# A three-part reordering of a two-block kernel: first norm with tokens on partitions, head products by rows, layer norm beside the gate tiles

## What is computed

```python
n = _rms(h, norm_mix_w[l])              # h: 528 x 1024
z = n @ w_in[l]                         # q, k, v, glu, g_att, g_conv
o = _diff_attention(q, k, v, lam, cid)  # 8 heads, two maps each, block-causal
y_att = _rms(o, subln_w[l]) * (1.0 - lambda_init)
u = glu[..., :CONV_CH] * jax.nn.sigmoid(glu[..., CONV_CH:])
u = _causal_dwconv(u, conv_dw_w[l], conv_dw_b[l])          # 31 taps
u = jax.nn.silu(_layernorm(u, conv_ln_w[l], conv_ln_b[l]))
y_conv = u @ w_conv_out[l]
m = jax.nn.sigmoid(g_att) * y_att + jax.nn.sigmoid(g_conv) * y_conv
h = h + m @ w_out[l]
h = h + conv_ffn(_rms(h, norm_ffn_w[l]))                   # then the second block
```

## Time and profile before

| | |
|---|---|
| median of 3 runs | 1731.55 us (1729.71 to 1734.51) |
| profiled execution | 1731.61 us, of it the span 1729.8 |
| TensorE busy | 1600.2 us, 93% |
| VectorE busy | 1166.5 us, 67% |
| ScalarE busy | 682.9 us, 39% |
| start, to the third chunk of products | 62.5 us |
| one turn of the heads | 36.8 us |
| turns 8 and 9, to the first chunk of w_conv_out | 426.3 to 520.2 us |

### The profile page before, as it was taken

One profiled execution on the slowest core, in us unless ns is written; L12 is line 12 of the kernel. 1 busy time (PEld: TensorE's weight loads), 2 busy tenths in 40 slices (PEclk: granted clock), 3 DMA queues, 4 the chain that ended last, 5 costly groups with the idle time before them and its releaser, 6 DMA issues.

```text
span 1729.8 us, 25539 instructions
## 1 busy us (share of the span) xinstructions
PE 1600.2 (93%) x9943; PEld 1408.4 (81%) x9943; DVE 1166.5 (67%) x1603; ACT 682.9 (39%) x1013; POOL 11.4 (1%) x26
## 2 busy tenths in 40 slices
PE   5997999999879999999999977979986899999996
PEld 4997889898779999999988866757865688888885
DVE  5889877876435578777764479855537887777334
ACT  3221455545453344433433344533633433343232
POOL 0000000000000000000000020000000000000000
PEclk8999999999999999999999998889998999999997
DMA  4232221121112323333223431312111333332331
GB/s 135 74 97 59 67 71 50 50 72 51 49 49 74 98 75 96 97 97 88 66 84 100 108 86 30 71 49 61 50 49 51 95 97 97 94 86 65 95 96 49
DMA packets 261145, 131.02 MB, mean 76 GB/s; under 512 B 21056, under 2 KB 259524, under 8 KB 261076
## 3 DMA queue, kind: packets, MB, share of 16 engines
q1 hardware_dynamic: 260692, 129.87, 27.2%
q0 software_dynamic: 384, 0.20, 0.0%
HBM read 127.95 MB, written 2.10 MB: 75 GB/s over the span
## 4 chain that ended last, share of the span: by engine, by line
PE 79%; DVE 14%; ACT 5%; issue 1%; DMA 0%; SPq 0%; DVEq 0%; ACTq 0%
PE psP L609 31%; PE psS L609 19%; PE psP L672 14%; PE psP L629 4%; DVE conv L1745 2%; DVE wl L1665 2%; PE psP L783 1%; DVE sc L2012 1%; DVE m L2011 1%; PE psS L745 1%; ACT wh L1175 1%; PE psP L1040 1%; PE psP L887 1%; PE psP L781 1%; DVE mT L2254 1%
## 5 line engine op out<-in xcount | busy, mean ns | idle before, releaser
L1665 DVE TENSOR_TENSOR wl<-raw,wh 128x2048 fp32r<-128x2048 f32 x130 | 297.9, 2291 | 151.8 <-ACT wh L1175 149.8
L609 PE MATMUL psP<-xh,wh 128*128 128x264 f32 (+2 forms) x1328 | 333.0, 316 | 27.7 <-DVE wl L1665 11.0
L609 PE MATMUL psP<-xl,wh 128*128 128x264 f32 (+2 forms) x1328 | 325.8, 310 | 0.0
L609 PE MATMUL psP<-xh,wl 128*128 128x264 f32 (+2 forms) x1328 | 325.6, 310 | 0.0
L1175 ACT ACTIVATE wh<-raw 128x2048 fp32r<-128x2048 f32 x130 | 248.5, 1911 | 98.4 <-PE psP L672 49.8
L609 PEld LDWEIGHTS psP<-xh,wh 128*128 128x128 f32 x1328 | 218.8, 193 | 48.8 <-issue 17.0
L609 PEld LDWEIGHTS psP<-xl,wh 128*128 128x128 f32 x1328 | 219.6, 192 | 12.5 <-issue 0.2
L609 PEld LDWEIGHTS psP<-xh,wl 128*128 128x128 f32 x1328 | 218.3, 192 | 12.5
L609 PE MATMUL psS<-xh,wh 128*128 128x258 f32 (+2 forms) x720 | 180.2, 312 | 0.4 <-DVE wl L1665 0.4
L1745 DVE SCALAR_TENSOR_TENSOR conv<-u,cdw,conv 128x516 f32<-128x516 f32 x232 | 175.1, 755 | 6.9
L609 PE MATMUL psS<-xh,wl 128*128 128x258 f32 (+2 forms) x720 | 179.7, 311 | 0.0
(11 more groups left out here) (400 smaller groups left out, 2335.9 us busy)
## 6 DMA issues: line engine op xcount, KB each, us to landing
raw<-in_w_in_dram SPq DMA_DIRECT2D x76, 512.0 KB, 5.0
raw<-in_w_up_dram SPq DMA_DIRECT2D x44, 512.0 KB, 4.7
raw<-in_ffn_up_dram SPq DMA_DIRECT2D x44, 512.0 KB, 4.5
raw<-in_w_out_dram SPq DMA_DIRECT2D x16, 512.0 KB, 4.8
raw<-in_w_down_dram SPq DMA_DIRECT2D x16, 384.0 KB, 3.5
raw<-in_ffn_down_dram SPq DMA_DIRECT2D x16, 384.0 KB, 3.4
raw<-in_w_down_dram SPq DMA_DIRECT2D x16, 320.0 KB, 3.9
raw<-in_ffn_down_dram SPq DMA_DIRECT2D x16, 320.0 KB, 3.9
```

The costliest lines, as they stand in the source:

```text
L609: ins = mm(ps[0:rows, a, 0:nn], W[:, s, half, k, 0:rows], Y[:, k, c0 + a * nn:c0 + (a + 1) * nn], start=(k == 0 and p == 0), stop=(k == KT ...
L1665: V.tensor_tensor(wl[:, n % 2], raw[:, n % 2], wh[:, n % 2].bitcast(f32), ALU.subtract).then_inc(s_lo, 1)
```

## The change

- **First norm.** Each token tile of 128x1024 (tokens on partitions) is squared and summed along its row by ScalarE, which also takes the root; VectorE inverts one column and scales the row (`xn`). TensorE transposes the normed tokens (`normed_tokens`, three tiles ahead) and, apart from them, the raw ones (`raw_tokens`) for `hT`. ScalarE copies the high part out of PSUM with the weight as scale; VectorE takes the low part from PSUM too. Chunk 0's weights are split in two halves of four k each. Chunk 0's products are written out with the transposes between the k steps. Raw tokens 2 and 3 are transposed behind chunk 0. Chunk 1's transfer comes ahead of the constants; the weight row is loaded alone at first.
- **Constants** are transposed between the two halves of chunk 1 and copied in the first gated unit, which has no taps now; its ten taps come at the end (the turns' quotas are as before, so two are left in turn 8). Lambda's exponential and two VectorE steps come after the eighth unit.
- **Head products.** In `scores` both maps' products first, then both masks, then both meta products. In `outputs` the 16-row products first (meta output, then the four t), then the ten over 128 keys, ending the group once.
- **Layer norm.** The centring in turn 8 is moved behind maximum 3 on VectorE, the squares on ScalarE behind the emptying of tiles 1 and 2. The total is taken before tile 1 of turn 9, the root together with the head's root, reciprocal and products behind it, the Silus before tile 2 is emptied, and the high parts as the last tile releases each k of `xh`. From the last tile of turn 8 on, tiles alternate between psP[0] and psS[1].

The diff, cut to its core:

```diff
-            sp.dma_start(mrow[:], A["meta_tokens"]).then_inc(s_xin, 16)
+            sp.dma_start(wrow[:], A["norm_mix_w"][0].rearrange("(g p) -> g p", p=128)).then_inc(s_wm, 16)
+            sp.dma_start(mrow[:], A["meta_tokens"]).then_inc(s_min, 16)
             for t in range(TT):
-                sp.dma_start(xrow[:, t, :], x[128 * t:128 * (t + 1), :]).then_inc(s_xin, 16)
+                sp.dma_start(xrow[:, t, :], x[128 * t:128 * (t + 1), :]).then_inc(s_xin[t], 16)
             G = 3 * D
             pair(w_in, 0, None, 0, G, G + D)
+            pair(w_in, 1, None, 0, G + 128, G + D + 128)
...
             inputs()
-            pair(w_in, 1, None, 0, G + 128, G + D + 128)
...
+            def raw_tokens(t, ps):
+                for k in range(KT):
+                    ins = tr(ps[:, k // 4, 128 * (k % 4):128 * (k % 4 + 1)], xrow[:, t, 128 * k:128 * (k + 1)], ident[:])
+                ins.then_inc(s_xt, 1)
+
+            def normed_tokens(k):
+                if k >= 3:
+                    pe.wait_ge(s_nl, k - 2)
+                for t in range(TT):
+                    ins = tr(scores_ps[:, k % 3, 128 * t:128 * (t + 1)], xn[:, t, 128 * k:128 * (k + 1)], ident[:])
+                ins.then_inc(s_nt, 1)
...
+            for t in range(2):
+                pe.wait_ge(s_xin[t], 16)
+                raw_tokens(t, psP[t])
+            pe.wait_ge(s_xn, TT + 1)
+            for k in range(3):
+                normed_tokens(k)
+            pe.wait_ge(s_hm, 2)
+            pe.wait_ge(s_ms, 2)
+            pe.wait_ge(s_l0, 1)
+            for k in range(KT):
+                if k == KT // 2:
+                    pe.wait_ge(s_lo, 1)
+                pe.wait_ge(s_nl, k + 1)
+                for half in range(2):
+                    for p, (W, Y) in enumerate(((wh, xh), (wh, xl), (wl, xh))):
+                        for a in range(2):
+                            ins = mm(psP[half][:, a, 0:HT], W[:, 0, half, k, :], Y[:, k, a * HT:(a + 1) * HT],
+                                     start=(k == 0 and p == 0), stop=(k == KT - 1 and p == 2))
+                    if k == KT - 1:
+                        ins.then_inc(s_mm, 1)
+                if k + 3 < KT:
+                    normed_tokens(k + 3)
...
+            for t in range(2, TT):
+                pe.wait_ge(s_xin[t], 16)
+                raw_tokens(t, psS[t - 2])
+            pe.wait_ge(s_hm, 3)
+            project(ALLP[2], 1, 0, X, 0, HT, None)
 
             pe.wait_ge(s_in, N_IN)
-            tr(psS[0][:, 0, 0:V_ROWS], vrow[:], ident[0:V_ROWS, 0:V_ROWS])
+            pe.wait_ge(s_ed, CREDIT + 1)
...
+            pe.wait_ge(s_hm, 4)
+            project(ALLP[3], 1, 1, X, 0, HT, None)
...
-                for m in range(2):
-                    P = slice(64 * m, 64 * m + 64)
+                maps = [slice(64 * m, 64 * m + 64) for m in range(2)]
+                last = []
+                for m, P in enumerate(maps):
                     q = qkv[P, a % 2, 0, NM + 128 * t:NM + 128 * (t + 1)]
                     K = qkv[P, a % 2, 1, :]
                     if t < 3:
                         bank = scores_ps[:, 2 * (t % 2) + m, :]
                         mm(bank[:, 0:PW[t]], q, K[:, 0:PW[t]], start=True, stop=False)
-                        last = bank[:, PW[t] - 64:PW[t]]
+                        last.append(bank[:, PW[t] - 64:PW[t]])
                     else:
-                        bank = None
                         mm(scores_ps[:, 2 * m, 0:HT], q, K[:, 0:HT], start=True, stop=True)
                         mm(scores_ps[:, 2 * m + 1, 0:HT], q, K[:, HT:T], start=True, stop=False)
-                        last = scores_ps[:, 2 * m + 1, HT - 64:HT]
-                    ins = mm(last, mki[P, :], mkk[P, :], start=False, stop=True)
-                    if t == 0:
-                        ins = mm(bank[0:NM, PW[0]:PW[0] + NM], qkv[P, a % 2, 0, 0:NM], K[:, 0:NM], start=True, stop=True)
+                        last.append(scores_ps[:, 2 * m + 1, HT - 64:HT])
+                for m, P in enumerate(maps):
+                    ins = mm(last[m], mki[P, :], mkk[P, :], start=False, stop=True)
+                if t == 0:
+                    for m, P in enumerate(maps):
+                        ins = mm(scores_ps[0:NM, m, PW[0]:PW[0] + NM], qkv[P, a % 2, 0, 0:NM], qkv[P, a % 2, 1, 0:NM], start=True,
+                                 stop=True)
                 ins.then_inc(s_qk, 1)
...
+                o = [psP[1][:, 0, 128 * t:128 * (t + 1)] for t in range(TT)]
+                mm(psP[1][0:NM, 1, 0:128], aTm[:, S:S + NM], vtok[0:NM, TT, :], start=True, stop=True)
                 for t in range(TT):
-                    o = psP[1][:, 0, 128 * t:128 * (t + 1)]
-                    mm(o, aTm[:, 128 * t:128 * (t + 1)], vtok[0:NM, TT, :], start=True, stop=False)
+                    mm(o[t], aTm[:, 128 * t:128 * (t + 1)], vtok[0:NM, TT, :], start=(t == 0), stop=False)
+                for t in range(TT):
                     for j in range(t + 1):
-                        mm(o, aT[:, j, 128 * t:128 * (t + 1)], vtok[:, j, :], start=False, stop=(j == t))
-                mm(psP[1][0:NM, 1, 0:128], aTm[:, S:S + NM], vtok[0:NM, TT, :], start=True, stop=True).then_inc(s_at_o, 1)
+                        ins = mm(o[t], aT[:, j, 128 * t:128 * (t + 1)], vtok[:, j, :], start=False, stop=(j == TT - 1))
+                ins.then_inc(s_at_o, 1)
...
+                elif h == NH and q < 3:
+                    project(psP[0], n, half, X, C3, H3, 1)
                 else:
-                    project(psP[0], n, half, X, C3, H3, 1)
+                    if h == NH:
+                        pe.wait_ge(s_ex, 4 * NH)
+                    project((psP[0], psS[1])[q % 2], n, half, X, C3, H3, 2, release=s_xr if h > NH and q == 3 else None)
...
+                if h == NH + 1:
+                    pe.wait_ge(s_os, NH)
+                    total(1, psP[1], H3, 16)
...
+            pe.wait_ge(s_ea, evacuated(2 * N_CO - 2)[1])
             pe.wait_ge(s_rt, 2)
+            project_pair(ALLP[0:2], N_CO, X, C3, H3, None, (s_nl, 8))
+            pe.wait_ge(s_ea, evacuated(2 * N_CO - 1)[1])
             pe.wait_ge(s_oy, NH)
-            wide(N_CO, X, C3, H3, 4, ready=(s_nl, 8))
+            for half in range(2):
+                project(ALLP[2 + half], N_CO + 1, half, X, C3, H3, None)
+            for c in range(2, 4):
+                for half in range(2):
+                    project(ALLP[2 * (c % 2) + half], N_CO + c, half, X, C3, H3, 4)
...
+            for t in range(TT):
+                act.wait_ge(s_xin[t], 16)
+                own(fn(flat, xrow[:, t, :], ACT.Square, accum_out=rcol[:, t:t + 1]))
+                fn(rcol[:, t:t + 1], rcol[:, t:t + 1], ACT.Sqrt, bias=eps6[:], scale=1.0 / D).then_inc(s_rs, 1)
...
+            def first_hi(j):
+                act.wait_ge(s_raw[0], 32)
+                fn(wh[:, 0, :, 4 * j:4 * j + 4], raw[:, 0, :, 4 * j:4 * j + 4], ACT.Copy).then_inc(s_hi if j else s_h0, 1)
+
+            def normed_hi(k):
+                act.wait_ge(s_nt, k + 1)
+                fn(xh[:, k, NM:T], scores_ps[:, k % 3, :], ACT.Copy, scale=vmix[:, k:k + 1]).then_inc(s_nh, 1)
+
+            act.wait_ge(s_mx, 1)
+            fn(xh[:, :, 0:NM], mw[:], ACT.Copy).then_inc(s_ms, 1)
+            first_hi(0)
+            normed_hi(0)
+            normed_hi(1)
+            first_hi(1)
+            for k in range(2, KT):
+                normed_hi(k)
...
+                if b == NH - 1:
+                    root(1, psP[1], H3, eps5)
...
+                    centred_squares(0, 4)
+                if h == NH + 1:
+                    for k in range(KT):
+                        act.wait_ge(s_ln, k + 1)
+                        fn(conv[:, k, :], conv[:, k, :], ACT.Silu, scale=vec[:, V_LNW + k:V_LNW + k + 1],
+                           bias=vec[:, V_LNB + k:V_LNB + k + 1]).then_inc(s_lu, 1)
                 empty(h, 2)
                 if 0 <= a < NH:
                     copy_probs(a, 2)
+                if h == NH:
+                    centred_squares(4, KT)
                 if h == NH + 1:
-                    root(1, psS[1], H3, eps5)
+                    for k in range(KT):
+                        if k < KT - 1:
+                            act.wait_ge(s_xr, k + 1)
+                        else:
+                            act.wait_ge(s_mm, 2 * N_CO)
+                        act.wait_ge(s_lu, k + 1)
+                        fn(xh[:, k, C3:T], conv[:, k, :], ACT.Copy).then_inc(s_nh, 1)
...
+            def norm_tokens(j, n_, src, dst):
+                dve.wait_ge(s_rs, j + 1)
+                r = rcol[0:n_, (j - 1) % (TT + 1):(j - 1) % (TT + 1) + 1]
+                own(V.reciprocal(r, r))
+                V.tensor_scalar(dst, src, r, None, ALU.mult).then_inc(s_xn, 1)
+
+            def keep_tokens(t, ps):
+                dve.wait_ge(s_xt, t + 1)
+                V.tensor_copy(hT[:, :, NM + 128 * t:NM + 128 * (t + 1)], ps[:].rearrange("p a (b c) -> p (a b) c", c=128)).then_inc(s_hm, 1)
...
```

(17 more changed lines are left out.)

188 lines of the change are left out of this document (96 added, 92 removed).

## The result

The changed kernel takes 1687.92 us (median of 4 runs, 1686.59 to 1688.78), the kernel before beside it 1732.91 (4 runs, 1729.71 to 1734.51). The ratio is 0.974, 95% interval 0.9725 to 0.9759. The forecast was 1693.4 in 1684 to 1707. The profiled execution is the slowest of the four, 1688.78 with a span of 1687.0; against the profiled one of before (1731.61, span 1729.8) that is 42.8 less, where 38.2 was forecast.

What follows compares the result with a forecast made beforehand. TensorE, busy 93% of the span, was taken as the bound. Start 10.5, lambda -0.4, first head 0.3, six head turns 10.8 and gate tiles with layer norm 17.0 sum to 38.2: 1731.6 to 1693.4 us, range 1684 to 1707.

Steps and rivals of the forecast that it cites:

- the two new waits: Last head and gate tiles: TensorE idle 3.4 us before the conv means and 2.9 before the last head's transposes.
- Start, 10.5: New first norm: third chunk of products begins at 52.0 instead of 62.49, 10.5 us gained, bounds 8 and 13.5.
- Lambda -0.4: After the last gated unit: moved taps and lambda steps on VectorE, there the chain, cost 0.4 us.
- first head +0.3: First head, held by VectorE, gains only 0.3 us.
- Scores 0.61 + 0.33: Scores in each head: maps side by side save 0.61 us at t=0 and 0.33 at t=3; t=1, t=2 nothing.
- Outputs 1.22: Outputs in each head: grouping products by row count, ten changes becoming three, saves about 1.2 us, bounds 0.8 and 1.4.
- The 0.36 taken off for new waits in a head: Each head turn: VectorE running late makes TensorE wait before gate tiles, cutting the 2.16 us saving to 1.8.
- Turns 8 and 9, 17.0: Last head, gate tiles, layer norm: 17.0 us gained after 0.9 low-clock cost for each new wait; bounds 13 and 19.5.
- 1: Rival for the heads: ScalarE and VectorE set the turn, which shortens only 0.6 us; 1700.6 us, chance 0.14.
- 2: Rival for the start: each root needs table loads, 10.2 us in all, so first norm isn't quicker; 1703.6, chance 0.04.
- 3: Rival for head products: maps already overlapped wherever possible and grouping outputs gives half; 1702 us, chance 0.06.
- 4: Rival, slower: waits at every head tile drop TensorE's clock, +43 us over 28 tiles; 1736.5 us, chance 0.02.

Runs made afterwards that it cites:

- e8: Changed kernel with every 128x1024 token tile scaled twice by VectorE at the start; 1690.93 us, ratio 0.9765.
- e9: Changed kernel with the copy of raw token tile 1 moved from VectorE to ScalarE; 1688.33 us, ratio 0.9748.
- e3: Changed kernel with the layer-norm part undone, including the gate tiles' accumulators; start and head products stay new; 1702.54 us, ratio 0.9843.
- e2: Kernel before with the new order of the scores alone; 1723.86 us, ratio 0.9965.
- e1: Kernel before with the new scores and outputs and nothing else of the change; 1714.41 us, ratio 0.991.
- e13: Changed kernel with the outputs' products in two pairs of blocks, two more changes between row counts per head; 1691.88 us, ratio 0.9781.
- e14: Changed kernel with the first map's mask back between the maps for t=1 and t=2; 1688.89 us.
- e7: e6 with one tap more at the end of each head turn (HEAD_TAPS 21, not 20); 1677.67 us, ratio 0.9686.
- e11: e6 with ten taps fewer in turn 0 of the heads and two more in every turn (HEAD_TAPS 22); 1672.35 us, ratio 0.9654.
- e6: Changed kernel with the convolution's centring and squares moved earlier on VectorE and ScalarE, four and four; 1681.93 us, ratio 0.972.

## Why the forecast was right, and by which steps not

The forecast named the stages, the two new waits and the sign, and missed the profiled time by 4.6 us. That is the sum of errors that partly cancel: +4.8 in the start, +0.4 in the first head and lambda, +1.9 in the six turns, -3.1 in turns 8 and 9, +0.6 in the rest. So the closeness of the total is in part luck.

- **Start, 10.5, measured 15.3 where the forecast looked (third chunk).** The mechanism held, the terms were too large. Scaling 1024 columns was put at 1.1 to 1.2, from products whose two inputs are tiles; with a column of numbers as the second input it takes 0.75, where the split of 1024 columns, with two tile inputs, takes 1.22. The Trainium skill, VectorE: DVE Perf Modes, section The perf-mode tier table, lets a float32 operation with one tensor input in SBUF run at twice the rate and one with two not; the two rows agree, and I had not weighed it. A ScalarE tile was put at 1.55 and takes 1.37. With the queue shorter, tile 3 was normed at 14.1 instead of 17.5, and the first products came at 17.4 instead of 21. Then one cold k step of 2.14 instead of one or two of 2.6 to 2.9: chunk 0 took 14.5 and not 16. e8 shows the first of these to be on the chain; e9 shows that the chain has only 0.6 to give before TensorE's own transposes take over. The gain of 15.3 lies above my bound of 13.5.
- **Start, what it moves.** "The turns' quotas are as before, so two are left in turn 8" was seen, and its wait of 3.4 was put into the stage of the layer norm. e3 shows it as a debt of the start part, 5.3. Net of it the start gives 10.0, so the 10.5 forecast for the part as a whole comes near it by luck.
- **Lambda -0.4 and first head +0.3**: forecast together -0.1, measured +0.3. No run separates the two.
- **Scores 0.61 + 0.33**: measured 0.92 (e2). **Outputs 1.22**: measured 1.26 (e2 to e1), by changes (e13). The rows of before carried both to 0.05, though the count of seven changes in the outputs doesn't hold (six or eight, as said at e13). The rule of the Trainium skill, TensorE: Matmul & The Clock Gate, section Part 3: Packing small matmuls (strictly first in, first out), would have made it 2.8 a head; e14 shows no difference between the two orders, so here the measurement stands against it. The Trainium skill, TensorEngine Tiling, section Key Properties, says that a change of tiling mode drains the engine; e13's 0.19 to 0.2 per change agrees with a cost at each one.
- **The 0.36 taken off for new waits in a head**: this step failed. I had VectorE 0.5 late and TensorE waiting 0.3 before the third tile. In five of the six turns TensorE's idle time is 0.28, as before, and each gave 2.2. Only in the first of the six does such a wait stand, 0.48, and it gave 1.7. VectorE had more room than its one idle time in front of that maximum showed; e7 and e11 put it between one tap and two (0.79 each).
- **Turns 8 and 9, 17.0, measured 13.9.** Waits of 3.4 and 2.9 were forecast, 3.40 and 3.65 measured. The failed term is the low clock behind them, 0.9 each. It was read from a tile (7.59 against 6.05) and then cut to half for no reason that a row gave. Measured are 1.8 on the means (8.9 against 7.14 in e7; 2.9 in e6's trace) and 3.1 on the outputs (6.75 against 3.66 in e6): 3.1 more than forecast, as much as the whole error of this term. The second wait, 0.75 longer than forecast, is made up for by the tiles before it, which were done some 0.6 sooner than forecast.
- **Rivals.** 1 falls with e1's turn of 34.64. 2 falls with the rows of ScalarE: no table load stands between square and root. 3 falls with e2 (scores 0.92) and e1 beside it (outputs 1.26). 4 falls because no head tile of the six turns shows a low clock (granted 1.00).

What stays open is why one and the same wait of 3.40 cost 1.8 in some traces and 2.9 in others, and why the end of the kernel moves by 1 to 2 us between profiled executions of the same code (from the end of the first pair on, 1193.5 in e1 and 1195.4 before). Neither was tried.

## What to carry to other kernels

Price a wait on TensorE with what runs behind it at the lower clock: here 3.4 to 3.7 us of idle time cost 1.8 to 3.1 more, and removing one of them gave 6.6 at its place and not 3.5 (6.0 by the medians of the kernel). When an order is changed by quotas, follow each leftover to the place where it lands; two taps left over cost 5.3, a third of what the start had won. And where a group alternates between row counts, count the changes: here 0.19 to 0.2 us each, while a mask between two maps on different rows cost nothing.

## What the runs showed of the hardware

- VectorE scales a 128x1024 float32 tile from SBUF by a column in 0.75 us; it copies as many elements out of PSUM in 1.22, and subtracts two such tiles in SBUF in 1.22 (the changed kernel).
- Products of the two row halves overlap across a mask that stands between them in program order: 0.73 for four records of 272 columns, in either order (e14).
- A change between 16 and 128 rows costs TensorE 0.19 to 0.2 us (e13).
- Behind 3.40 us of idle time the same 32 products took 8.9 us in four traces and 10.0 to 10.1 in two; with no wait they took 7.14 (e7).
- After 3.65 us of idle time TensorE was granted 0.56 over the next 7.74 us, in which it was busy all the time with small products; after 7.83 the next tile took 7.63 instead of 6.1.
